# First mixer of a fused block: side work placed between the items of its dense stage

## The reference, cut to what matters

```
z = rms_norm(x) @ w_in                       # 512 x 3088: q, k, v, o, 16 gates, gu, gv
qk = silu(depthwise_conv5([q, k]) + conv_b)
i_f, f_f, i_b, f_b = gates + gate_b          # 4 heads each
b  = cumsum(log_sigmoid(f)) within the sequence, forwards and backwards
r  = i - b                                   # per key position
h  = mlstm(qk, v, b, r), both directions     # weights exp(r[s] + b[t] - max) * (q . k)
y_mlstm = sigmoid(o) * (h * rsqrt(mean(h*h per head)) * g_head)
gu = gelu(gu);  gv = layer_norm(gelu(gv)) * ln_v_g + ln_v_b
sp = w_s[g] @ gv[chunk, :, g] + b_s          # mixing over the 128 positions of a chunk
y_gmlp = gu * sp
x += concat([y_mlstm, y_gmlp]) @ w_out
```

## Time and profile before

| | |
|---|---|
| median of three runs | 3036.12 us |
| the profiled execution | 3035.32 us |
| its span, first to last instruction | 3033.6 us |
| TensorE busy in the span | 2463.5 us (81%) |
| VectorE, ScalarE, GpSimd busy | 1301.4, 889.5, 407.8 us |
| mean granted TensorE clock | 0.900 |
| first mixer, from the norm to the last item of the output projection | about 27 to 367 us |

### The profile page before, as it was taken

How to read it: one execution, slowest core, us unless ns; L and a number is a source line. 1 busy time by engine, 2 the same in 40 slices (tenths; PEclk the granted TensorE clock), 3 DMA queues, 4 the chain that set the end, 5 groups by cost and what they waited for, 6 DMA issues and landing times. The chain is left out here.

```text
span 3033.6 us, 50648 instructions
## 1 busy us (share of the span) xinstructions
PE 2463.5 (81%) x18120; PEld 1934.1 (64%) x18121; DVE 1301.4 (43%) x2776; ACT 889.5 (29%) x1677; POOL 407.8 (13%) x718
## 2 busy tenths in 40 slices
PE   4975799888888886869899869983959989869882
PEld 4963788854444446757677857763848667757661
DVE  4437345521111115634753544335644754453334
ACT  2233234211111113144532313322233633213221
POOL 1000000022122210000000134442000000024333
PEclk9988899889999998979999869996979999969996
DMA  3200242679999954022121479993212212459993
GB/s 127 85 1 1 70 139 58 278 319 403 411 410 404 395 219 152 29 70 61 44 62 52 155 291 345 381 363 137 70 35 70 61 51 63 164 197 374 383 388 140
DMA packets 209305, 565.80 MB, mean 187 GB/s; under 512 B 26598, under 2 KB 170598, under 8 KB 184592
## 3 DMA queue, kind: packets, MB, share of 16 engines
q1 hardware_dynamic: 191104, 538.73, 47.8%
q0 software_dynamic: 18064, 25.23, 2.5%
HBM read 560.46 MB, written 36.18 MB: 197 GB/s over the span
## 5 line engine op out<-in xcount | busy, mean ns | idle before, releaser
L1027 PE MATMUL ps<-m_gate_up,e_xT 128*64 128x256 f32 x1088 | 271.4, 413 | 64.1 <-DMA m_gate_up<-in_w_gate_up 57.9
L1027 PEld LDWEIGHTS ps<-r_gate_up,e_xT 128*64 128x64 f32 x2272 | 264.3, 143 | 91.3 <-issue 87.7
L1027 PE MATMUL ps<-r_gate_up,e_xT 128*64 128x128 f32 x2272 | 276.8, 283 | 41.4 <-DMA r_gate_up<-in_w_exp_gate_up 34.2
L1029 PE MATMUL ps<-r_gate_up,e_xT 128*64 128x128 f32 x2272 | 276.9, 283 | 0.0
L1027 PEld LDWEIGHTS ps<-m_gate_up,e_xT 128*64 128x64 f32 x1088 | 160.6, 150 | 177.0 <-issue 113.3
L1181 DVE TENSOR_TENSOR e_hid<-e_silu,ps 64x128 f32<-64x128 f32 (+1 forms) x210 | 70.2, 335 | 473.3 <-ACT e_silu L1069 469.3
L1029 PE MATMUL ps<-m_gate_up,e_xT 128*64 128x256 f32 x1088 | 271.5, 413 | 0.0
L1029 PEld LDWEIGHTS ps<-r_gate_up,e_xT 128*64 128x64 f32 x2272 | 264.3, 143 | 0.0
L1069 ACT ACTIVATE e_silu<-ps 64x128 f32<-64x128 f32 (+1 forms) x210 | 63.6, 303 | 654.7 <-PE ps L1029 654.7
L2195 PE MATMUL ps<-t_hT,t0a_t0g_w 128*128 128x512 f32 x768 | 199.4, 411 | 4.6 <-DVE t0a_t0g_w L2217 2.4
L2195 PE MATMUL ps<-t_hT,t1a_t1g_w 128*128 128x512 f32 x768 | 198.1, 409 | 4.6 <-DVE t1a_t1g_w L2217 2.4
(11 more groups left out here) (647 smaller groups left out, 4793.9 us busy)
## 6 DMA issues: line engine op xcount, KB each, us to landing
m_gate_up<-in_w_gate_up SPq DMA_DIRECT2D x32, 4096.0 KB, 39.0
r_gate_up<-in_w_exp_gate_up SPq DMA_DIRECT2D x64, 2048.0 KB, 31.1
m_down<-in_w_down SPq DMA_DIRECT2D x32, 2048.0 KB, 38.9
r_down<-in_w_exp_down SPq DMA_DIRECT2D x64, 1024.0 KB, 34.0
t0a_t0g_raw<-in_w_in SPq DMA_DIRECT2D x32, 512.0 KB, 3.8
t1a_t1g_raw<-in_w_in SPq DMA_DIRECT2D x32, 512.0 KB, 3.8
mixw_raw<-in_w_in SPq DMA_DIRECT2D x10, 1024.0 KB, 5.2
xaw_raw<-in_w_kv_x SPq DMA_DIRECT2D x8, 1024.0 KB, 5.4
```

What stands on the lines that cost most here:

```text
L1027: nc.tensor.matmul(ps_gu[q][0:SLOTS], xT[:, c, :], ring.gu[s][:, 0, c, span], start=c == 0, stop=c == DC - 1)
L1029: last = nc.tensor.matmul(ps_gu[q][SLOTS:P], xT[:, c, :], ring.gu[s][:, 1, c, span], start=c == 0, stop=c == DC - 1)
```

## The change

`dense` gets hooks: `act_side(act, c)` behind ScalarE's outputs of chunk c, `pe_side(pe, n)` behind item n on TensorE, and `banks`, the length of the ring of PSUM banks. The mixer calls it with 5 banks, so that banks 5 to 7 are free for other products.

The order of the chunks becomes q and k, o with gates (chunks 4, 5; items 8 to 15), gv (6, 7; items 16 to 23), gu (8, 9; items 24 to 31), v (10, 11; items 32 to 39, now emptied by ScalarE). In the diff below, what is left out of `by_dve` is: the taps (as before), the gate bias, the LayerNorm's statistics and its normalizing, gain and bias, the copies of the running sums out of PSUM, and the position products' `(product + b_s) * gu`. What is left out of `by_act` are Abs, Exp and Ln, and of `by_pe` the matmuls themselves (16 short ones for the running sums in bank 7, the products with `w_sT`, the spreading of r). The separate steps before attention, the LayerNorm stage and the position-product stage are gone; their instructions stand in the hooks. Attention writes its heads into `y` and not into `raw`; the spread rows lie in `raw`. The product of o with `g_head` moves from the head norm into chunk 6's side. The head norm takes its squares, mean, root and products by token tile.

```diff
-def dense(nc, name, k, chunks, items, raw_ring=3, side=None, before=None):
+def dense(nc, name, k, chunks, items, raw_ring=3, side=None, before=None, act_side=None, pe_side=None, banks=8):
...
-                    if i >= 8:
-                        pe.wait_ge(emptied[items[i - 8].engine], nth[i - 8])
+                    if i >= banks:
+                        pe.wait_ge(emptied[items[i - banks].engine], nth[i - banks])
...
                     last.then_inc(bank_full, 1)
+                    if pe_side is not None:
+                        pe_side(pe, i)
...
+                    if act_side is not None:
+                        act_side(act, c)
...
+            hs = y[:, :, 0:512]
+            rows = raw[:, :, 0:S]
...
+            BANKS = 5
+            mix_bank = lambda t: ps[:, BANKS + t % 2, :]
+            row_bank = lambda j: ps[:, BANKS + 1 + j % 2, :]
...
+            def by_dve(dve, c, emptied):
...
+                if c == 6:
+                    dve.wait_ge(emptied["act"], 12)
...
+                    vec.tensor_copy(pair(f), g4[:, :, 1::2, :]).then_inc(f_ready, 1)
+                    for t in range(TT):
+                        vec.tensor_tensor(o[:, t, :], o[:, t, :], k["rows"]["g_head"], ALU.mult)
+                if c == 8:
+                    dve.wait_ge(ln_ready, 1)
+                    vec.scalar_tensor_tensor(ls[:], f[:], 0.0, l1[:], ALU.min, ALU.subtract).then_inc(ls_ready, 1)
+                    dve.wait_ge(emptied["act"], 20)
...
+                    vec.tensor_scalar(root[:, 0], mv[:, :, 1], 1e-5, None, ALU.add).then_inc(mean_ready, 1)
+                if c == 9:
+                    dve.wait_ge(root_ready, 1)
...
+                    last.then_inc(gv_ready, 1)
+                    dve.wait_ge(summed, 1)
...
+                    vec.tensor_tensor(pair(r), g4[:, :, 0::2, :], pair(b), ALU.subtract).then_inc(r_ready, 1)
+                if c == 10:
+                    dve.wait_ge(silu_ready, 2)
+                    dve.wait_ge(emptied["act"], 28)
+                    for t in range(TT):
+                        dve.wait_ge(mixed, t + 1)
...
+                        last.then_inc(gated, 1)
+                    for j in range(8):
+                        dve.wait_ge(rows_full, j + 1)
+                        vec.tensor_copy(rows[:, j, :], row_bank(j)).then_inc(rows_ready, 1)
+
+            def by_act(act, c):
+                if c in (5, 6):
+                    act.wait_ge(tapped, 20 * (c - 4))
+                    for q in range(4 * (c - 5), 4 * (c - 4)):
+                        last = sca.activation(qk[:, q, :], acc[:, q, :], ACT.Silu, bias=col("conv_b")[:, q:q + 1])
+                    last.then_inc(silu_ready, 1)
+                if c == 7:
+                    act.wait_ge(f_ready, 1)
+                    act.preload_act_table_set("natural_log_exp_and_others")
...
+                if c == 8:
+                    act.wait_ge(mean_ready, 1)
+                    sca.activation(root[:, 1], root[:, 0], ACT.Sqrt).then_inc(root_ready, 1)
+
+            def by_pe(pe, n):
+                if n == 29:
+                    pe.wait_ge(ls_ready, 1)
...
+                for t in {32: (0, 1), 33: (2, 3)}.get(n, ()):
+                    if t == 0:
+                        pe.wait_ge(gv_ready, 1)
+                    if t >= 2:
+                        pe.wait_ge(gated, t - 1)
...
+                    last.then_inc(mixed, 1)
+                for j in range(2 * (n - 34), 2 * (n - 33)) if 34 <= n <= 37 else ():
+                    if j == 0:
+                        pe.wait_ge(r_ready, 1)
+                    if j < 2:
+                        pe.wait_ge(gated, TT)
+                    else:
+                        pe.wait_ge(rows_ready, j - 1)
...
+                    last.then_inc(rows_full, 1)
...
             with Stage(nc, "mixg") as st:
...
+                        for t in range(TT):
+                            for h in range(H):
+                                last = sca.activation(junk[:, h], hs[:, t, h * P:(h + 1) * P], ACT.Square,
+                                                      accum_out=ss[:, t, 0, h:h + 1])
+                            link(last)
+                            act.sem_inc(squared, 1)
+                            if t:
+                                root(t - 1)
+                        root(TT - 1)
...
+                        mean(0)
+                        for t in range(TT):
+                            if t + 1 < TT:
+                                mean(t + 1)
+                            dve.wait_ge(root_ready, t + 1)
...
-        ln_rows(nc, "mixl", lambda t: gv[:, t, :], lambda t: gv[:, t, :], TT, 512, 1e-5,
...
-        with Stage(nc, "mixp") as st:
...
```

More of the change, by code:

```diff
@@ L210, in _ @@
                             dve.wait_ge(bank_full, i + 1)
-                            it.out(nc.vector, ps[0:it.rows, i % 8, 0:it.n]).then_inc(emptied["dve"], 1)
+                            it.out(nc.vector, ps[0:it.rows, i % banks, 0:it.n]).then_inc(emptied["dve"], 1)
                     if side is not None:
@@ L1428, in taps @@
                                                          ALU.add).then_inc(tapped, 1)
-            dense(nc, "mixw", k, chunks, items, raw_ring=2, side=taps,
-                  before=TurnSplit(nc, k, TT, lambda t, c: y[:, t, c * P:(c + 1) * P], hT, DC, col("g_mix")))
-            with nc.Block() as block:
-                @block.scalar
-                def _(act):
-                    for c in range(8):
-                        sca.activation(qk[:, c, :], acc[:, c, :], ACT.Silu, bias=col("conv_b")[:, c:c + 1])
-                @block.vector
-                def _(dve):
-                    vec.tensor_tensor(gates[:], gates[:], k["rows"]["gate_b"].unsqueeze(1).to_broadcast([P, TT, 16]), ALU.add)
@@ new lines, in by_dve @@
+                if c == 9:
+                    dve.wait_ge(root_ready, 1)
+                    link(vec.reciprocal(root[:, 2], root[:, 1]))
+                    for t in range(TT):
+                        last = vec.tensor_scalar(gv[:, t, :], gv[:, t, :], mv[:, t, 0:1], root[:, 2, t:t + 1],
+                                                 ALU.subtract, ALU.mult)
+                    link(last)
+                    for t in range(TT):
+                        last = vec.tensor_tensor(gv[:, t, :], gv[:, t, :], k["ln_v"][:, 0], ALU.mult)
+                    link(last)
+                    for t in range(TT):
+                        last = vec.tensor_tensor(gv[:, t, :], gv[:, t, :], k["ln_v"][:, 1], ALU.add)
+                    last.then_inc(gv_ready, 1)
+                    dve.wait_ge(summed, 1)
+                    vec.tensor_copy(b[:, :, 0:4], forward)
+                    link(vec.tensor_copy(b[:, :, 4:8], backward))
+                    vec.tensor_tensor(pair(r), g4[:, :, 0::2, :], pair(b), ALU.subtract).then_inc(r_ready, 1)
@@ new lines, in mixer_one @@
+            dense(nc, "mixw", k, chunks, items, raw_ring=2, side=by_dve, act_side=by_act, pe_side=by_pe, banks=BANKS,
+                  before=TurnSplit(nc, k, TT, lambda t, c: y[:, t, c * P:(c + 1) * P], hT, DC, col("g_mix")))
+            units = []
+            for h in range(H):
+                for t in range(TT):
+                    n = (h * TT + t) * 2
+                    hi = (t + 1) * P
+                    off = S - P - t * P
+                    units.append(Unit(h, t, 0, hi, n, k["mask_le"][:, off:off + hi], rows[:, h, 0:hi], b[:, t, h:h + 1]))
+                    lo = t * P
+                    units.append(Unit(h, t, lo, S, n + 1, k["mask_ge"][:, S - P:S - P + S - lo], rows[:, 4 + h, lo:],
+                                      b[:, t, 4 + h:5 + h], add=True))
@@ L1501, in _ @@
[L1501 to L1504 removed]
+                            if t + 1 < TT:
+                                mean(t + 1)
+                            dve.wait_ge(root_ready, t + 1)
+                            link(vec.reciprocal(ss[:, t, 3], ss[:, t, 2]))
```

148 lines of the change are left out of this document (70 added, 78 removed).

## The result

The changed kernel takes 2990.52 us (median of 4 runs, 2988.36 to 2998.82) against 3035.53 us before (4 runs, 3032.71 to 3040.34): a ratio of 0.9855, 95% interval [0.9832, 0.9878].

A forecast was written before the change was run, and what follows sets the result against it. TensorE was taken to bound the dense stage, with serial short steps on the path around attention. Gains of 12.59 + 0.43 + 1.4 + 20.28 = 34.7 us gave a forecast of 3001.4 us, range 2995.5 to 3008.5.

The forecast's parts named there:

- The walk through the dense stage: Dense stage's token part: TensorE gains 12.37 us of work; no chunk, bank or operand is late, with 2.6 to 2.9 to spare.
- Rival 2: Dense stage: work queued ahead of splits is 5 us late at three places, TensorE idles 7 us, total 3008; chance 0.2.
- rival 3: Dense stage: five hooks each hold ScalarE until TensorE drains, making the kernel slower than before, 3060 us; chance 0.03.
- Attention's first matmul: End of the dense stage: attention's engines start at 193.62 where they started at 206.85, 13.23 us gained.
- The two exits: Around the head norm: one exit fewer before it gains 0.43 us; only a double exit left behind it gains 20.28.
- the head norm: Between attention and projection: working by tile ends near 11.7 us instead of 13.13, gain 1.4, bounds 0 and 2.5.
- the projection: Output projection: first matmul stays 8.58 us behind the first transpose, clock still 0.50 at 321 to 323; no gain.
- Rival 1: Output projection starts warm: cold transposes raise the clock and it holds, gaining 2.9 us, total 2998.5; chance 0.3.
- The table: Attention's start: the Exp table must be loaded again, costing 1.28 us partly covered, so 0.64 lost; bounds 0 and 1.28.
- Allowance behind the mixer: Program after the first mixer: the gain passes through unchanged; later clock ramps fall at other moments, 2 us allowed each way.
- Theory A: From the experiments: time differences behind the mixer are chance of single executions, clock ramps falling differently.
- B: From the experiments: differences behind the mixer follow from the change, through when the rest starts or the clock state it finds.

The follow-up runs named there:

- chained_squares: The changed kernel with each of the head norm's 16 squares waiting for the one before, the rest still by token tile; 2993.14 us, ratio 0.9869.
- old_head_norm: The changed kernel with the head norm of before: all squares chained, then one mean, one root and the products; 2992.83 us, ratio 0.987.
- scans_rows_apart: The changed kernel with gate bias, logarithm, running sums and row spreading put back as separate steps ahead of attention; 3006.64 us, ratio 0.992.
- both_early_two: The changed kernel with two output-weight chunks fetched during the head norm and the Exp table loaded after chunk 9's outputs; 2984.77 us, ratio 0.9844.
- ln_products_apart: The changed kernel with LayerNorm and position products put back as stages between head norm and output projection; 3015.4 us, ratio 0.9944.
- both_early_warm: As both_early_two, with 40 unused TensorE products of constants added during the head norm; 2991.17 us, ratio 0.9866.
- both_early: The changed kernel with two output-weight chunks fetched during the head norm and the Exp table loaded behind v's last output; 2990.52 us, ratio 0.986.

## Why the prediction was wrong

**What held.** The walk through the dense stage held at every step: TensorE busy 103.93 us of the forecast 104, no stall, the added instructions 1.70 for the sums, 3.4 for the products and 6.8 for the spreading, 11.9 together; the token part is 12.4 us longer, as forecast (12.37), the last 0.5 us lying in the items between them. The low part of chunk 7 ended at 120.04 (forecast 120.4), the root came at 147.37 (147.9), gv was ready at 158.81 (159.3) and asked for at 161.46 (161.9). Rival 2 (covers too thin) and rival 3 (a hook that drains TensorE) find no row: no matmul of that stage waits. Attention's first matmul was forecast at 193.6 and came at 193.31, since the token part began 0.38 us earlier than before (88.17 against 88.55). The two exits came to 0.40 and 20.19 of 0.43 and 20.28. That the removed steps are worth what was priced is shown by putting them back: 11.8 us at the mixer's end for scans and rows, 16.87 for LayerNorm and products, of which 1.8 and 1.4 us are a longer projection; silu alone was not put back.

**The step that failed: the head norm.** "Gain 1.4; bounds 0 and 2.5", from squares of 1.75 us a tile. That pace came from a row of the kernel before, in which each square waits for the one before it; the diff links only the last of a tile. Unlinked they follow each other in 0.29 us, not 0.43, a tile takes about 1.4 us with its handoff, and the gain is 3.2, outside the bound. chained_squares is the head norm that the forecast priced, and took 11.60 us. The term was mis-sized by 1.8.

**The step that was decided the wrong way: the projection.** "At 321 to 323 the clock is still 0.50; I leave that loss as it is." Rival 1, at 0.3, is what happened: the transposes start cold, take 5.13 us, the clock rises among them, and it holds through the shorter gap. It was priced at 2.9 us and the stage gained 1.99, but only 1.15 of them are the clock: the first matmul came 7.74 us behind the first transpose and not 8.58, which is 0.84, and from there to the mixer's end it took 49.71 us and not 50.85. All three profiles of the changed kernel take 49.7 for that; the second of before takes 50.2, so that the warm clock is worth 0.5 to 1.15. TensorE's rows, before and after, show why it is less than 2.9:

```profile
317.28 48.91 PE L153 MATMUL ps<-mixo_w,mix_hT 128*128 128x256 f32 x384 [4.89 <-DVE mixo_w L191]
```

```profile
282.69 44.15 PE L153 MATMUL ps<-mixo_w,mix_hT 128*128 128x256 f32 x366 [0.25 <-DVE mixo_w L195]
```

At full clock TensorE waits 0.25 us for VectorE's low part behind each of the first three groups of six matmuls; at half clock it is slow enough never to wait. The splits, and not the clock, set that pace, and part of the loss to the clock was covered by them. In old_head_norm the clock was 0.50 for the first 3.3 us of the matmuls, and from the first of them to the mixer's end it took 49.71 as well.

That the clock holds is not certain from the gap alone: in old_head_norm and scans_rows_apart the transposes were cold as well (5.90 and 5.56 us) and the clock still fell once the matmuls had begun. The time from the first transpose to the first split adds scatter of its own, 5.0 to 7.3 us over the profiles that fetch the weights in this stage. Above 5.1 the split waits for the weights to land; why they land up to 2 us later in some executions stays open.

**The table.** Its load costs 0.61 at attention's first Exp, as forecast (0.64), but attention gave most of it back by its end; both_early_two shows 0.2 us left to win. From its first matmul to its end it took 66.14 us before and 66.15 after. The forecast carried the loss through, 0.6 too much.

**Allowance behind the mixer.** The forecast took one profile of before for the base and 2 us either way for later ramps. Its base, the median 3036.12 us, lies 3.7 above the mean of all 61 runs of before, and the rest scatters by 15 us over profiles. The stated range does not follow from its bounds either: added up they give 2996.4 to 3011.6 and not 2995.5 to 3008.5, and rival 1's 2.9 us, held to be 0.3 likely, are in neither. Of the miss, 3001.4 - 2990.5 = 10.9 us, 4.6 are the mixer (1.8 head norm, 2.0 projection, 0.6 table, 0.3 the earlier start of the token part, less 0.1 at the exits), 3.7 the height of the base, and 41.7 - 39.2 = 2.5 the rest of the program. Whether these last 2.5 us, two standard errors of the gain, are chance or belong to the change stays open: the two profiles of before have 2665.5 and 2664.5, and twelve others a mean of 2660.4, but with single ones at 2665.6 and 2669.9. Theory A carries most of the 7.6; of B only that much could be left, and the delays of 18 and 50 us show no dependence on the moment of the start. The long rest of ln_products_apart, in its four runs too, is explained by neither.

The Trainium skill ("ScalarE: Activation LUTs", section What ACT_TABLE_LOAD costs) adds a drain of about 1380 ns to each load. The trace does not agree: the load of 1.28 us starts at 193.27 and Exp at 194.56, 1.29 later.

## What to carry to other kernels

A pace read from a chained group is no price for the same instructions unchained: look in the diff at what is linked, and price the group again. Moving short serial steps between the items of a stage that TensorE bounds costs what TensorE issues for them (12.4 us here) and saves their whole old length (25.56 us ahead of attention, where 206.85 - 180.10 = 26.75 became 193.31 - 192.12 = 1.19, and 0.40 + 20.19 behind it), as long as each engine's own queue has its answer ready before TensorE asks; walk that item by item. A clock that is slow where another engine sets the pace costs less than half the time it lasts (here 1.15 us for the 5.9 at 0.50 from 317.28 to 323.2): price it from the waits of the full-speed case. For a change of 1% in a program of 3 ms, give the base and the scatter of the clock their own term in the range before the mechanism's bounds.

## What the runs showed of the hardware

- The granted clock can fall to 0.50 while TensorE works, a little after a gap: in scans_rows_apart at 293 to 295 with TensorE busy 2.00 of 2.00 us, and in both_early_warm at 274 to 276, after products that ended 1.95 us before the transposes.
- 32 transposes of 128x128 took 3.68 us where products at full clock preceded them and 5.1 to 6.2 us from a cold start, with the clock reaching 1.00 among them (0.67 at 273 to 275 and 1.00 at 275 to 277 in the changed kernel).
- A table load behind the last instruction ahead of a meeting of all engines lengthens the meeting by all of its time: TensorE idle for 2.48 us ahead of attention in both_early and 1.19 in the changed kernel, for a load of 1.28.
- Squares with an accumulator, 128x128, start every 0.29 us unchained and every 0.43 chained. Unchained, the next square begins while the accumulator read of 0.19 us still runs (read at 260.43, next square at 260.53 in the changed kernel); chained, it begins after the read (read at 260.19, next square at 260.41 in chained_squares).
